# Expert results by way of DRAM and a gather per token, in place of a place matrix, and a new order of turns, downs and residuals

## The reference, cut to what matters

```
def grouped_moe(h, router_w, router_bias, w_in, w_out, sh_in, sh_out):
    scores = jax.nn.sigmoid((t @ router_w).astype(jnp.float32))
    sel = scores + router_bias
    grp_score = lax.top_k(sel.reshape(-1, 4, 4), 2)[0].sum(-1)
    best = jnp.argmax(grp_score, axis=-1)                  # one group of 4 experts per token
    _, idx = lax.top_k(jnp.where(in_group, sel, -jnp.inf), 2)
    w = jnp.take_along_axis(scores, idx, axis=-1); w = w / w.sum(-1, keepdims=True)
    gates = jnp.sum(jax.nn.one_hot(idx, 16) * w[..., None], axis=1)
    hid = swiglu(jnp.einsum('td,edf->tef', t, w_in))       # 1024 -> 2 x 256 per expert
    routed = jnp.einsum('tef,efd->td', hid * gates[..., None], w_out)   # 256 -> 1024
    shared = swiglu(t @ sh_in) @ sh_out
    return (routed + shared).reshape(bsz, n, d)
```

## Time and profile before

| | |
|---|---|
| median of 3 runs | 1302.78 us (1299.45 to 1303.5) |
| profiled execution | 1298.22 us |
| its span, first to last instruction | 1296.4 us |
| mean granted TensorE clock | 0.936 |
| busy: PE, DVE, ACT, POOL | 1106.5, 674.0, 650.7, 542.1 us |
| expert loop of layer 0 (5 blocks) | 397.5 to 603.1 us |
| expert loop of layer 1 (4 blocks) | 1106.7 to 1272.8 us |

### The profile page before, as it was taken

One profiled execution on the slowest core, in us unless ns is written; L12 is line 12 of the kernel. 1 busy time (PEld: TensorE's weight loads), 2 busy tenths in 40 slices (PEclk: granted clock), 3 DMA queues, 4 the chain that ended last, 5 costly groups with the idle time before them and its releaser, 6 DMA issues.

```text
span 1296.4 us, 16671 instructions
## 1 busy us (share of the span) xinstructions
PE 1106.5 (85%) x5822; PEld 868.7 (67%) x5822; DVE 674.0 (52%) x1055; ACT 650.7 (50%) x1162; POOL 542.1 (42%) x359
## 2 busy tenths in 40 slices
PE   4799978898888888989789999767767988888898
PEld 1585653448556677767579999656657954666777
DVE  1322845343338777765566620366753133767783
ACT  2514513352515666766455443677654242566671
POOL 0431520024035545545236655356646403655550
PEclk9699999997998989999889999898989989989999
DMA  8643449940457889885213333455610316788981
GB/s 335 254 163 102 158 177 385 421 177 30 159 178 277 314 304 340 306 311 200 97 65 103 127 131 130 136 134 163 179 41 33 130 63 215 270 291 312 346 285 49
DMA packets 84238, 255.77 MB, mean 197 GB/s; under 512 B 7312, under 2 KB 39632, under 8 KB 71376
## 3 DMA queue, kind: packets, MB, share of 16 engines
q1 hardware_dynamic: 78496, 243.30, 52.6%
q0 software_dynamic: 2048, 6.37, 1.4%
q10 hardware_dynamic: 3632, 5.30, 1.2%
HBM read 242.57 MB, written 7.65 MB: 193 GB/s over the span
## 4 chain that ended last, share of the span: by engine, by line
PE 46%; issue 16%; POOL 15%; ACT 8%; DVE 7%; DMA 6%; POOLq 0%; SPq 0%; ACTq 0%; DVEq 0%
POOL wlo L727 10%; PE bank L1966 9%; PE bank L1967 8%; PE bank L1968 8%; POOL wlo L687 4%; PE bank L1990 3%; PE bank L2351 3%; DMA raw<-experts 3%; PE bank L2481 2%; PE bank L2047 2%; ACT seg L1251 2%; ACT whi L810 2%; DMA raw<-stream 1%; PE bank L2210 1%; DMA slot_rows<-tok_row,slot_of 1%
## 5 line engine op out<-in xcount | busy, mean ns | idle before, releaser
L687 POOL TENSOR_TENSOR wlo<-raw,whi 128x512 fp32r<-128x512 f32 x168 | 224.9, 1371 | 320.2 <-ACT whi L810 320.2
L1054 ACT CAST whi<-raw 128x1024 fp32r<-128x1024 f32 x216 | 226.1, 1052 | 106.9 <-DMA raw<-experts 57.4
L727 POOL TENSOR_TENSOR wlo<-raw,whi 128x1024 fp32r<-128x1024 f32 x72 | 198.8, 2762 | 159.7 <-ACT whi L1054 159.7
L1696 DVE TENSOR_TENSOR wlo<-raw,whi 128x1024 fp32r<-128x1024 f32 x144 | 226.4, 1598 | 49.8 <-ACT whi L1054 49.4
L1966 PE MATMUL bank<-hhi,whi 128*128 128x384 f32 (+1 forms) x504 | 175.5, 348 | 18.9 <-POOL wlo L687 8.9
L1967 PE MATMUL bank<-hlo,whi 128*128 128x384 f32 (+1 forms) x504 | 172.8, 343 | 0.0
L1968 PE MATMUL bank<-hhi,wlo 128*128 128x384 f32 (+1 forms) x504 | 172.5, 342 | 0.0
L1966 PE MATMUL bank<-whi,blk_hi 128*128 128x512 f32 x288 | 115.9, 403 | 4.7 <-issue 2.0
L1966 PEld LDWEIGHTS bank<-hhi,whi 128*128 128x128 f32 (+1 forms) x504 | 96.8, 192 | 30.2 <-POOL wlo L687 13.0
L1968 PE MATMUL bank<-whi,blk_lo 128*128 128x512 f32 x288 | 113.7, 395 | 0.0
L1967 PE MATMUL bank<-wlo,blk_hi 128*128 128x512 f32 x288 | 113.4, 394 | 0.0
(11 more groups left out here) (353 smaller groups left out, 2045.4 us busy)
## 6 DMA issues: line engine op xcount, KB each, us to landing
raw<-experts SPq DMA_DIRECT2D x216, 512.0 KB, 5.2
raw<-stream SPq DMA_DIRECT2D x61, 1024.0 KB, 4.8
modw<-core_mods SPq DMA_DIRECT2D x32, 1024.0 KB, 9.3
rowb<-acs_rows SPq DMA_DIRECT2D x48, 256.0 KB, 5.0
shared<-shared SPq DMA_DIRECT2D x6, 1024.0 KB, 7.7
h_next<-h_blk SPq DMA_DIRECT2D x9, 512.0 KB, 4.8
h_rows<-h_tok SPq DMA_DIRECT2D x6, 512.0 KB, 2.6
s<-s0T SPq DMA_DIRECT2D x8, 256.0 KB, 4.3
```

The costliest lines, as they stand in the source:

```text
L687: ins = pool.tensor_tensor(wlo[:, q % SPL, w], raw[:, pos % RAW, w], whi[:, q % SPL, w].bitcast(F32), ALU.subtract)
L727: pool.tensor_tensor(unit(wlo, j), unit(raw, j), unit(whi, j).bitcast(F32), ALU.subtract).then_inc(ls.e_lo[j % SLOTS], 1)
L1054: act.copy(unit(whi, j), unit(raw, j)).then_inc(ls.e_hi, 1)
L1696: dve.tensor_tensor(unit(wlo, j), unit(raw, j), unit(whi, j).bitcast(F32), ALU.subtract).then_inc(ls.e_lo[j % SLOTS], 1)
```

## The change

1. A block's result is copied by ACT as plain fp32 to one buffer `y_sb` and stored by an ACT DMA to rows of `y_rows` in DRAM (`result_out`). `yhi_e`, `ylo_e`, DVE's `result_lo` and POOL's two memsets go, with the waits for them.
2. After the loop POOL waits for the last store and fetches each token's row with three indirect DMAs into `y_tok`; PE turns them (24 transposes of 128 x 128) into the eight `comb` banks. `place`, `back` and the 96 matmuls per layer go.
3. Rows of blocks 3 to 5 of both `y_rows` are filled early in the program by two POOL DMAs of 1.5 MB out of x.
4. The loop: PE turns each expert before the down of the expert ahead of it, and both halves of the next block before down 2. ACT and DVE split expert 2's turned part right behind SiLU 3 or the gate product 3.
5. Before the loop: ACT splits the six first units ahead of block 0's rows, DVE mixes low parts and residuals ahead of block 0's low part, and PE turns block 0 after the fifth `shd` job instead of the sixth.

```diff
                 ls = loop_sems[layer]
...
-                finished(pool, JOB[f"shu{layer}_3"])
-                pool.wait_ge(place_ready, (TILES + 2) * (layer + 1))
-                pool.memset(ylo_e[:, MIN_BLOCKS:, :].bitcast(F32), 0.0).then_inc(pool_step, 1)
-                finished(pool, JOB[f"shd{layer}_{KC - 1}"])
-                pool.memset(yhi_e[:, MIN_BLOCKS:, :].bitcast(F32), 0.0).then_inc(pool_step, 1)
...
+                pool.wait_ge(ls.y_out, count * 16 + 16)
+                pool.sem_inc(pool_step, 1)
+                pool.wait_ge(pool_step, 2 * layer + 3)
+                for t in range(TILES):
+                    pool.indirect_dma_start(y_tok[:, t * D:(t + 1) * D], None, y_dram[layer][:, :],
+                                            bass.IndirectOffsetOnAxis(slot_of[:, t:t + 1], 0)).then_inc(y_in, 16)
...
+            low_to("aq01")
+            pool.wait_ge(x_in, 16)
+            for layer in range(DEPTH):
+                pool.dma_start(y_dram[layer][MIN_BLOCKS * P:, :].rearrange("(p r) f -> p (r f)", p=P),
+                               x[:, :, :].rearrange("p k n -> p (k n)")).then_inc(rows_out, 16)
...
-                def result_hi(it):
+                def result_out(it):
                     act.wait_ge(ls.e_used[(GRP_UNITS - 1) % SLOTS], it * SLOT_USES + (1 + SLOT_USES))
+                    act.wait_ge(ls.y_out, it * 16 + 16)
                     for half in range(2):
-                        act.copy(yhi_e[:, bass.ds(it, 1), half * 512:(half + 1) * 512],
-                                 bank[Y_BANK + half][:, :].unsqueeze(1)).then_inc(ls.y_hi_ready, 1)
+                        act.copy(y_sb[:, half * 512:(half + 1) * 512], bank[Y_BANK + half][:, :]).then_inc(ls.y_ready, 1)
+                    act.wait_ge(ls.y_ready, it * 2 + 2)
+                    act.dma_start(y_dram[layer][bass.ds(it * P, P), :], y_sb[:, :]).then_inc(ls.y_out, 16)
...
                     silu(it, 3)
+                    turned_hi(it, 2)
                     split_e(it, 23)
                     if not last:
                         split_e(it + 1, 0)
-                    turned_hi(it, 2)
-                    if not last:
-                        split_e(it + 1, 1)
-                        split_e(it + 1, 2)
                     turned_hi(it, 3)
-                    if not last:
-                        split_e(it + 1, 3)
                     blk_part(it + 1)
                     if not last:
-                        split_e(it + 1, 4)
-                        split_e(it + 1, 5)
-                    result_hi(it)
+                        for j in range(1, SLOTS):
+                            split_e(it + 1, j)
+                    result_out(it)
...
-                blk_part(0, FIRST_PERM)
                 act.wait_ge(groups_ready, layer + 1)
                 last = last_block(act)
                 for j in range(SLOTS):
                     split_e(0, j)
-                act.wait_ge(pool_step, 1 + 3 * (layer + 1))
+                blk_part(0, FIRST_PERM)
...
-                for j in range(2):
+                for j, kcs in ((0, ()), (1, (0, 1)), (3, (2, 3)), (4, (4,))):
                     low_e(0, j)
-                for kc in range(KC):
+                    for kc in kcs:
+                        residual(JOB[f"shd{layer}_{kc}"], layer, 5, kc)
+                blk_part(0, FIRST_PERM)
+                for kc in range(5, KC):
                     residual(JOB[f"shd{layer}_{kc}"], layer, 5, kc)
-                for j in range(2, SLOTS):
-                    low_e(0, j)
...
                     up(2)
-
+                    turn(1)
                     down(0)
-                    turn(1)
                     up(3)
+                    turn(2)
                     down(1)
-                    turn(2)
-
+                    turn(3)
                     pe.wait_ge(ls.next_in, it * 16 + 16)
                     turn_block(h_next, 0)
+                    turn_block(h_next, 1)
                     down(2)
-                    turn(3)
-                    turn_block(h_next, 1)
                     down(3)
...
+                pe.wait_ge(y_in, 16 * TILES * (layer + 1))
+                for kc in range(KC):
+                    dst = opened(JOB[f"comb{layer}_{kc}"])
                     for t in range(TILES):
+                        ins = pe.transpose(dst[:, t * P:(t + 1) * P], y_tok[:, t * D + kc * P:t * D + (kc + 1) * P],
+                                           k("ident"))
```

More of the change, by code:

```diff
@@ L116 @@
 _KATT = [("block", 128), ("rot", 128), ("cos", 256), ("sin", 256)]
-_KMOE = [("slots", MAX_BLOCKS * P), ("before", 128), ("blocks", 8), ("tokid", TILES), ("following", MAX_BLOCKS)]
+_KMOE = [("before", 128), ("blocks", 8), ("tokid", TILES), ("following", MAX_BLOCKS)]
 _KSSD = [("upto", 128), ("since", 128)]
@@ L192, in moe @@
             shu[:1] + [f"rank{layer}"] + shu[1:] + numbered(f"shd{layer}_", KC))
-        add(numbered(f"back{layer}_", MAX_BLOCKS) + numbered(f"comb{layer}_", KC))
+        add(numbered(f"comb{layer}_", KC))
     add(names)
@@ L356, in build @@
         shared = nc.alloc_sbuf_tensor_at("shared", [P, 3, PIECE], F32, offset=low)
-        my = Map(low)
-        yhi_e = my.put("yhi_e", [MAX_BLOCKS, D], F32R)
-        assert my.at <= free
         my = Map(free)
-        ylo_e = my.put("ylo_e", [MAX_BLOCKS, D], F32R)
+        y_sb = my.put("y_sb", [D])
         mm = Map(max(my.at, norm_end))
@@ L448, in build @@
         h_dram = [nc.dram_tensor(f"h_rows{layer}", [NTOK, D], F32).ap() for layer in range(DEPTH)]
+        y_dram = [nc.dram_tensor(f"y_rows{layer}", [MAX_BLOCKS * P, D], F32).ap() for layer in range(DEPTH)]
         row_dram = [nc.dram_tensor(f"slot_rows{layer}", [MAX_BLOCKS * P, ROW_W], F32).ap() for layer in range(DEPTH)]
@@ L493, in __init__ @@
                     own("turned"), own("ht_hi_ready"), own("ht_lo_ready"))
-                self.y_hi_ready, self.y_lo_ready = own("y_hi_ready"), own("y_lo_ready")
+                self.y_ready, self.y_out = own("y_ready"), own("y_out")
         loop_sems = [LoopSems(layer) for layer in range(DEPTH)]
@@ L699, in moe @@
                 ls = loop_sems[layer]
-                pool.wait_ge(place_ready, (TILES + 2) * layer + 2)
-                pool.wait_ge(rows_out, 16 * DEPTH + 16 * TILES * layer)
+                pool.wait_ge(place_ready, 2 * layer + 2)
+                pool.wait_ge(rows_out, 32 * DEPTH + 16 * TILES * layer)
                 for t in range(TILES):
@@ L709, in moe @@
                 pool.tensor_copy(tok_of[:, :], slot_row[:, :, PER_GRP]).then_inc(pool_step, 1)
-                pool.wait_ge(pool_step, 3 * layer + 2)
+                pool.wait_ge(pool_step, 2 * layer + 2)
                 pool.wait_ge(tok_out, 16 * TILES * (layer + 1))
@@ L1120, in moe @@
                 one_block(last, True)
-                for b_ in range(MAX_BLOCKS):
-                    n = JOB[f"back{layer}_{b_}"]
-                    finished(act, n)
-                    took(act.copy(back[:, b_, :], bk(n)[:, 0:NTOK]), n)
                 if layer < DEPTH - 1:
@@ L1663, in find_places @@
                 dve.tensor_copy(slot_of[:, :], nums[:, 5, 0:TILES]).then_inc(place_ready, 1)
-                for t in range(TILES):
-                    dve.tensor_scalar(place[:, t, :], km("slots"), nums[:, 5, t:t + 1], None, ALU.is_equal).then_inc(
-                        place_ready, 1)
             def moe(layer):
@@ L1710, in turned_lo @@
                         ls.ht_lo_ready, 1)
-                def result_lo(it):
-                    for half in range(2):
-                        part = (slice(None), bass.ds(it, 1), slice(half * 512, (half + 1) * 512))
-                        dve.wait_ge(ls.y_hi_ready, it * 2 + (half + 1))
-                        dve.tensor_tensor(ylo_e[part], bank[Y_BANK + half][:, :].unsqueeze(1), yhi_e[part].bitcast(F32),
-                                          ALU.subtract).then_inc(ls.y_lo_ready, 1)
                 def one_block(it, last):
@@ L1739, in one_block @@
                     hidden(it, 3)
+                    turned_lo(it, 2)
                     low_e(it, 23)
@@ L2249, in moe @@
                 dst = opened(n)
-                pe.wait_ge(place_ready, (TILES + 2) * layer + 1)
+                pe.wait_ge(place_ready, 2 * layer + 1)
                 pe.wait_ge(kmoe_in, 16 * (layer + 1))
@@ L2670, in constants @@
     kcum = np.stack([r > c, r < c], axis=1).astype(f)
-    kmoe = np.concatenate([rows(np.arange(MAX_BLOCKS * P).astype(f)), (r < c).astype(f),
+    kmoe = np.concatenate([(r < c).astype(f),
                            rows(np.arange(8).astype(f)),
```

43 lines of the change are left out of this document (11 added, 32 removed).

## The result

The changed kernel took 1283.57 us (median of 4 runs, 1280.15 to 1286.07) against 1301.12 (1298.68 to 1303.5): ratio 0.9864, 95% interval 0.9829 to 0.9898. The gain is 17.5 us, or 1.4%; 38.5 were forecast. The profiled execution took 1286.07, its span is 1284.2.

The account below looks back on a forecast made before the run. PE was taken as the spine, with the DMA's floor deciding the middle blocks. Gains of 13.7, 12.4, 2.0, 9.2, 2.7 and 0, less 1.5, made 38.5 us and a median of 1264; range 1245 to 1288 for 8 in 10.

Parts of the forecast that it names:

- The loop's order: Five middle blocks of the loops: DMA floor 38.1 us plus 0.7 gives 38.8 each, 13.7 us gained.
- First and last blocks: Loop ends: first blocks take what a middle one takes, 12.4 us gained; last ones lose small waits, 2.0 gained.
- Ahead of the loops: Before both loops: PE starts 6.0 and 6.2 us earlier, less 1.5 per layer for loads beside the gather; 9.2 gained.
- my own mark of 7 us: Sign against the forecast: it would be wrong if the gathers take over 7 us.
- Behind the loops: After each loop, the round trip replaces matmuls and transposes: layer 1 gains 2.7 us, layer 0 gains 0 (-3.5 to 1.5).
- the last sentence there: Layer 0's tail: POOL's weight splits start 2.5 us later, hidden because PE is idle for the norm anyway.
- Early: Program start: two 1.5 MB fills near 71 us delay a weight piece; a loss of 1.5 us (0 to 4).
- the wait moves: Rival, loops: late SiLU or gate product stops PE at turn 3, middle blocks stay 41.5; 1284 us, chance 0.22.
- PE becomes the only bound: Rival, loops: the DMA keeps up, seven blocks at 36.3 us, 17.5 less; 1247 us, chance 0.14.
- The store breaks the ring: Rival, loops: ACT's store waits and extra bytes add 1.5 + 1.5 us a block, nine times; 1319 us, chance 0.07.
- nothing comes of it: Rival: gains ahead and tails as priced, nine blocks 1.5 us longer each by the bytes; 1306 us, chance 0.05.
- Sum: Whole kernel: terms add to 38.5 us gained, span 1296.4 becomes 1257.9, median 1264 us.

Follow-up runs that it names:

- the first trace: The profiled execution of the changed kernel from its first measurement, span 1284.2 us; median of those runs 1283.57 us.
- the second: The changed kernel run again unedited for another trace, span 1277.7 us; measured 1281.6 us, ratio 0.9847 to the kernel before.
- POOL held back: The changed kernel with POOL's low parts of the stream behind layer 0's gathers waiting until DVE's adds of the squares are done: 1281.6 us.
- the place matrix kernels: The kernel before with the new orders, place matrix and products kept, one or none of 24 low parts on POOL: 1231.4 and 1234.8 us.
- with the round trip: The changed kernel with squares behind layer 0's experts summed by matmuls, one or none of 24 low parts on POOL: 1244.2 and 1237.9 us.

## Why the prediction was right or wrong

**The loop's order: wrong in its bound.** "at 358 GB/s 38.1 us ... I add 0.7 and take 38.8" is the step that failed. I took a stretch with a DMA share of 0.97 for the DMA's limit. The same engines carried 390 GB/s in 34.9-us blocks when POOL's parts were cut, and half the bytes left the block at 40.1. What holds the block is the port, and DVE's own list of work behind it: 16 low parts of 1.21 and 8 of 2.4 us make 38.6 us if they exclude each other. In the timelines they nearly do. In the middle blocks of the changed kernel one engine or the other is at a low part for 36.4 to 37.3 us (36.3 to 36.5 with half the bytes), so some 2 us of the 38.6 overlap; and if DVE's other instructions are counted in, the two engines cover 38.2 to 39.4 us of blocks of 39.1 to 42.8. That my 38.8 is nearly the same number is chance, and what follows from it differs: I priced 1.5 us for a store and nothing for POOL. The middle blocks gave 5.4 instead of 13.7. The rows to see it by were there: a low part on DVE took 1.2 alone, and the page's group of 144 had a mean of 1.60:

```profile
L1696 DVE TENSOR_TENSOR wlo<-raw,whi 128x1024 fp32r<-128x1024 f32 x144 | 226.4, 1598 | 49.8 <-ACT whi L1054 49.4
```

I read past it because DVE was busy for only 31 of 42 us.

**First and last blocks.** The first ones gained 18.5, not 12.4, and take 35.8. Ahead of the loop DVE now does four low parts and POOL two, where it was four (three in layer 1) and none; so the first block holds 15 and 7 of them instead of 16 (17) and 9. That is port time spent before the loop begins. The last ones lost 4 to 5: they hold 13 and 7 instead of 12 and 7, which is one low part of 1.2 us. The rest of the loss is argued, not shown: before, PE's waits would have let low parts run ahead; PE now uses up that store, and the port decides to the end. I had priced each block by itself, though low parts move between blocks. All loops: 19.7 of 28.1 in the first trace, 18.4 in the second.

**Ahead of the loops: right.** 33.5 us from slots to loop became 28.2 in layer 1 (5.3, forecast 4.7) and 33.1 became 30.8 and 27.8 in layer 0. The gather is indeed seen later: PE stood for it, and its block landed beside the loads. From its issue it took 7.8 and 6.1 us in the first trace (layers 0 and 1), 5.5 and 6.2 in the second, and 4.2 before: 1.3 to 3.6 later, where 1.5 were priced, within 0 to 3 but for one. That is past my own mark of 7 us once, without harm to the sum.

```profile
394.14 1.19 PE L2224 MATMUL bank<-kon,h_blk 128*128 128x128 f32 x8 [3.12 <-DMA h_blk<-h_rows,tok_of]
```

**Behind the loops.** Layer 1 right: 13.1 us from the last matmul to the first transpose (12.7 forecast), each part within 0.4, the gain 2.0 to 2.5 (2.7). Layer 0 wrong: 0 was forecast, 10.2 lost. The store took 6.0 us to POOL's first gather, not 3.2, beside the next loads. Without the stand the chain would have held: it took 26.3 with POOL held back, and 25.9 before. What failed is the last sentence there: POOL's splits "start 2.5 us later with PE idle for the norm anyway: hidden". They cost the add 6.8 us in the first trace and 7.2 in the second. I looked for who waits for POOL's results, and not for who shares a port with it.

The Trainium skill ("SBUF — State Buffer", Who interferes with whom) states that a DVE instruction with two inputs in SBUF contends with a GpSimd instruction that reads SBUF, by an exclusive lock. The runs agree: 1.22 us with no expert part on POOL, 1.73 with eight of 24, 2.08 with the units there early. It is the rule I should have weighed instead of the one on queues. By it a loser would wait for one instruction of the other side; the add that stood for six of them is not explained by that.

**Early.** -1.5 forecast; about -1 by the slots of 20 traces of all kernels here. Right, though the first trace alone (-7.6) would have said otherwise.

**The rivals.** The time landed on "the wait moves", 1284, and its middle blocks (41.5) and tails (2.7, 0) were not what happened: it is near by compensation, not by mechanism. It did name a late gate product, and PE waited 9.1 us for these (11 times). At the one shown above, the two low parts ahead of it on DVE took 3.50 us together, 2.4 alone. "PE becomes the only bound" needed the port free; then it came true. "The store breaks the ring" and "nothing comes of it" priced the store's bytes, at 1.5 us and more a block; a second store cost under 1.

**Sum.** Of the 21 us missed, 8 to 10 are the loops (28.1 forecast, 19.7 and 18.4 in the traces) and 10 the stretch behind loop 0, some 7 of these the add. The rest is ahead of the slots and differs from trace to trace.

## What to carry to other kernels

Where DVE and POOL both subtract or multiply two operands in SBUF, add their times instead of overlapping them, and check the sum against the stage; the sign is a spread between the least and the mean duration of one instruction form. A second engine that needs twice as long for the same work and shares the port can cost more than it gives: taking six of its eight parts off gave more (25 us) than the change studied. Between one part and none the place matrix kernels show no difference, and with the round trip none was better (1237.9 against 1244.2). When a stage's instructions are moved on POOL, ask what runs on DVE at that time, not only who waits for POOL. And a high DMA share is a ceiling only if fewer bytes make the stage shorter; here they did not.

## What the runs showed of the hardware that was not expected

- A DVE add of two SBUF operands stood 7.3 to 7.8 us in all eight traces where the adds were kept and POOL went from the three gathers straight into twelve low parts, and it ended 0.4 us behind POOL's last in every one. In the four such traces where matmuls sum the squares, the first `gain` product stood instead, for 3.8 to 4.3 us, and ended with POOL's last. With POOL 4.8 us idle between gathers and low parts it took 1.24 and slowed POOL instead. In the kernel before, with the same row behind a wait for ACT, the adds took 0.55 to 1.6 and the row 16.6 us instead of 14.7. Why POOL doesn't give way behind its gathers stays open.
- The DMA carried 390 GB/s over a whole block, where 358 had looked like its limit.
- The result's store took 2.6 us to 7.4 to land (median 6.9), `h_rows` of the same size 3.4; but a second store a block cost under 1 us.
- The same code varies: in six traces whose loops are those of the changed kernel, single middle blocks lie between 38.5 and 42.8, and their sum over five between 199.6 and 202.5.
